# Block sums of the down-projection weights formed in HBM by accumulating DMAs, and sixteen chunk pairs as seven products in place of eight

## The reference, cut to what matters

```python
# first block, stage 0
u = causal_dwconv(h @ w_ffn_up[layer], ffn_conv_w[layer], ffn_conv_b[layer])
u_gate, u_val = jnp.split(u, 2, axis=-1)
x = x + (jax.nn.silu(u_gate) * u_val) @ w_ffn_down[layer]
# second block, stages 1 and 2
f_gate, f_up = jnp.split(h2 @ w_ffn_in[l], 2, axis=-1)
x = x + (jax.nn.silu(f_gate) * f_up) @ w_ffn_out[l]
```

## Time and profile before

| | |
|---|---|
| median of 3 runs | 1244.31 us (1244.18 to 1244.35) |
| profiled execution | 1244.18 us, its span 1242.9 us |
| PE busy | 1239.0 us (100%) |
| DVE, ACT, POOL busy | 957.8, 722.1, 422.0 us |
| DMA queue of SP | 232.67 MB, 53.4% of the 16 engines' time |
| granted TensorE clock | 1.0 throughout |

### The profile page before, as it was taken

The page is one execution under the profiler, slowest core; times in us unless marked ns, Lnnn a source line. Parts: engine busy times, 40 slices in busy tenths (PEclk is TensorE's granted clock), DMA queues, the critical chain, the costliest instruction groups (busy, mean ns, idle before and its releaser), DMA issues.

```text
span 1242.9 us, 17085 instructions
## 1 busy us (share of the span) xinstructions
PE 1239.0 (100%) x6634; PEld 1061.2 (85%) x6634; DVE 957.8 (77%) x1377; ACT 722.1 (58%) x1023; POOL 422.0 (34%) x338
## 2 busy tenths in 40 slices
PE   9999999999999999999999999999999999999999
PEld 8988788888888889888888888888988888888887
DVE  6875667677887478986878888986898597888895
ACT  7755545376765365577836555546457674655552
POOL 0010012039892069377420112008746750012100
PEclk9999999999999999999999999999999999999999
DMA  9753334555555448644554554465855454555442
GB/s 360 274 195 136 136 119 169 173 199 187 197 179 201 170 170 267 214 155 176 175 210 175 183 190 162 176 220 185 289 180 193 154 174 165 203 183 190 162 166 114
DMA packets 39008, 233.75 MB, mean 188 GB/s; under 512 B 4752, under 2 KB 5392, under 8 KB 13072
## 3 DMA queue, kind: packets, MB, share of 16 engines
q1 hardware_dynamic: 38928, 232.67, 53.4%
HBM read 225.31 MB, written 1.05 MB: 182 GB/s over the span
## 4 chain that ended last, share of the span: by engine, by line
PE 100%; DVE 0%; issue 0%; POOL 0%; POOLq 0%
PE ps L657 19%; PE ps L564 18%; PE ps L566 18%; PE ps L565 18%; PE ps L662 10%; PE ps L569 6%; PE ps L583 2%; PE ps L625 1%; PE ps L624 1%; PE ps L623 1%; PE ps L725 1%; PE ps L1209 1%; PE ps L700 0%; PE ps L893 0%; PE ps L810 0%; PE ps L811 0%
## 5 line engine op out<-in xcount | busy, mean ns | idle before, releaser
L1299 ACT ACTIVATE whi<-raw 128x2048 fp32r<-128x2048 f32 (+1 forms) x212 | 400.2, 1891 | 115.0 <-PE ps L566 101.5
L2052 DVE TENSOR_TENSOR wlo<-raw,whi 128x2048 fp32r<-128x2048 f32 x168 | 388.0, 2315 | 90.0 <-ACT whi L1299 89.3
L1885 POOL TENSOR_TENSOR wlo<-raw,whi 128x512 fp32r<-128x512 f32 x176 | 229.1, 1337 | 88.6 <-ACT whi L1299 85.6
L657 PE MATMUL ps<-hh,whi 128*128 128x512 f32 x1056 | 255.8, 391 | 0.0
L657 PEld LDWEIGHTS ps<-hh,whi 128*128 128x128 f32 x1056 | 193.0, 188 | 36.5
L564 PE MATMUL ps<-whi,hh 128*128 128x512 f32 (+1 forms) x504 | 201.3, 399 | 0.0
L566 PE MATMUL ps<-whi,hh 128*128 128x512 f32 (+1 forms) x504 | 195.5, 388 | 0.0
L565 PE MATMUL ps<-wlo,hh 128*128 128x512 f32 (+1 forms) x504 | 195.1, 387 | 0.0
L1857 POOL TENSOR_TENSOR st<-st,sm 128x1 f32<-128x1 f32 (+2 forms) x28 | 45.2, 1614 | 391.5 <-DVE st L2106 228.0
L662 PEld LDWEIGHTS ps<-hh,wlo 128*128 128x128 f32 x1056 | 137.8, 191 | 6.7
L662 PE MATMUL ps<-hh,wlo 128*128 128x256 f32 x1056 | 139.8, 282 | 0.0
(11 more groups left out here) (348 smaller groups left out, 2061.6 us busy)
## 6 DMA issues: line engine op xcount, KB each, us to landing
raw<-in_w SPq DMA_DIRECT2D x202, 1024.0 KB, 4.9
raw<-in_w SPq DMA_DIRECT2D x12, 256.0 KB, 6.7
gain<-in_bias SPq DMA_DIRECT2D x12, 256.0 KB, 5.0
kst<-kh SPq DMA_DIRECT2D x16, 128.0 KB, 2.8
qst<-qh SPq DMA_DIRECT2D x16, 128.0 KB, 2.3
raw<-in_w SPq DMA_DIRECT2D x2, 560.0 KB, 10.8
x<-in_x SPq DMA_DIRECT2D x4, 256.0 KB, 5.7
gain<-in_rows SPq DMA_DIRECT2D x2, 512.0 KB, 5.6
```

Of the source, the lines that this page charges most:

```text
L657: pe.op.matmul(o[:, :], wh[:, k, c], t.hh[:, k, :, :], start=k == 0, stop=False, skip_group_check=True)
L1299: act.op.activation(t.whi[i % NHI][:, c], t.raw[i % NRAW][:, c], ACT.Copy).then_inc(*at("act_hi", ("hi", i)))
L1885: pool.op.tensor_tensor(t.wlo[i % NRAW][:, half(k)], t.raw[i % NRAW][:, half(k)], t.whi[i % NHI][:, half(k)].bitcast(F32), ALU.subtract).t ...
L2052: dve.op.tensor_tensor(t.wlo[i % NRAW][:, c], t.raw[i % NRAW][:, c], t.whi[i % NHI][:, c].bitcast(F32), ALU.subtract).then_inc(*at("dve_lo ...
```

## The change

Sixteen pairs are made as seven products in place of eight: four in stage 0, five in stage 1, seven in stage 2. No weight sum is made by DVE. SP copies three of the four weight blocks of each pair from HBM to a tensor `sums` in HBM (two DMAs of 512 KB for a pair), and POOL issues accumulating DMAs of 256 KB that add blocks within HBM (four for a pair, in three steps with waits between them). They come in two batches: nine pairs (stages 0 and 1) with their copies ahead of the loads of chunks 16 to 24, and seven pairs (stage 2) with theirs ahead of the loads of the seven chunks from `pa0_0` on. The sum chunk of a pair is then loaded like any other, 1 MB, and of the pair's own chunk only three of four blocks are loaded, 0.75 MB. In stage 0 DVE makes the sums of `g` (`block_sums`) and their lower part, as POOL splits weights there.

```diff
+    def down(unit, name, layer):
+        n = int(unit[2])
...
+            plan.append((name, layer, cols((512, 512), (0, 512)) if c in SEVEN[n] else cols((0, 1024)), 2 * c, 2))
+            if c in SEVEN[n]:
+                plan.append((None, n, range(1024), 2 * c, 2))
...
-SEVEN = (1, 3, 5, 7)
+SEVEN = ((2, 3, 4, 6), (1, 2, 3, 4, 5), (1, 2, 3, 4, 5, 6, 7))
+BY_DVE = ((), (), ())
...
+FORMED = [i for i in sorted(SUMS) if PLAN[i][3] // 2 not in BY_DVE[PLAN[i][1]]]
+BATCH = [[i for i in FORMED if (PLAN[i][1] == 2) == late] for late in (False, True)]
+COPIES = {a + n: i for a, batch in zip((16, UNITS["pa0_0"][0]), BATCH) for n, i in enumerate(batch)}
...  sp_program
-        load(f"d_raw{i % NRAW}", t.raw[i % NRAW][:, 0:width(i)], src, ("raw", i))
+        c = slice(512 if i + 1 in FORMED else 0, width(i))
+        load(f"d_raw{i % NRAW}", t.raw[i % NRAW][:, c], src[:, c], ("raw", i))
+
+    def load_sums(i):
+        sp.wait_ge(*on("used", i - NRAW))
+        sp.wait_ge(*on("sums formed", int(i in BATCH[1])))
+        load(f"d_raw{i % NRAW}", t.raw[i % NRAW][:, :], d["sums"][FORMED.index(i)], ("raw", i))
+
+    def blocks_copied(i):
+        src = d["in_w"][OFFS[i - 1]:OFFS[i]].rearrange("(p n) -> p n", p=128)
+        for h in range(2):
+            load("d_copied", d["sums"][FORMED.index(i)][:, 1024 * h:1024 * h + 1024], src[:, 512 + 512 * h:1536 + 512 * h],
+                 *([("blocks copied", int(i in BATCH[1]))] * (h and i in (BATCH[0][-1], BATCH[1][-1]))))
...
-        if i not in SUMS:
+        if i in COPIES:
+            blocks_copied(COPIES[i])
+        if i in FORMED:
+            load_sums(i)
+        elif i not in SUMS:
             load_raw(i)
...  act_program, stage 0
+            if f % 2 and (f - 3) // 2 in SEVEN[n]:
+                sums_upper((f - 3) // 2)
...  pool_program
+    def added(sem, dst, src, *names):
+        pool.op.dma_start(dst, src, accum_op=ALU.add).then_inc(*at(sem, *names, by=16))
+
+    def first_sums(late):
+        pool.wait_ge(*on("blocks copied", late))
+        for i in BATCH[late]:
+            s = d["sums"][FORMED.index(i)]
+            first = d["in_w"][OFFS[i - 1]:OFFS[i]].rearrange("(p n) -> p n", p=128)[:, 0:512]
+            for j in range(2):
+                added("d_one", s[:, half(j)], first, *([("first sums", late)] * (j and i == BATCH[late][-1])))
+
+    def later_sums(late):
+        pool.wait_ge(*on("first sums", late))
+        for i in BATCH[late]:
+            s = d["sums"][FORMED.index(i)]
+            added("d_two", s[:, half(2)], s[:, half(0)], *([("second sums", late)] * (i == BATCH[late][-1])))
+        pool.wait_ge(*on("second sums", late))
+        for i in BATCH[late]:
+            s = d["sums"][FORMED.index(i)]
+            added("d_three", s[:, half(3)], s[:, half(2)], *([("sums formed", late)] * (i == BATCH[late][-1])))
...  behind the rope of kr, before the retention statistics
+    first_sums(0)
...  behind the retention statistics, before the powers of norm n1
+    later_sums(0)
...  behind the powers of the norm before stage 1, and around its g_sums
+        if l == 0:
+            first_sums(1)
+        for c in SEVEN[l + 1]:
             g_sums(l + 1, c)
+        if l == 0:
+            later_sums(1)
...  dve_program
-            if i + 1 in SUMS:
+            if i + 1 in SUMS and i + 1 not in FORMED:
                 weight_sums(i)
...
+            if n == 0 and f % 2 and (f - 3) // 2 in SEVEN[n]:
+                block_sums((f - 3) // 2)
+            if n == 0 and f % 2 == 0 and (f - 4) // 2 in SEVEN[n]:
+                c = (f - 4) // 2
+                lower([("g sums", n, c)], t.gsl[SEVEN[n].index(c)][:, :, :], t.gs[:, :, :],
+                      t.gsh[SEVEN[n].index(c)][:, :, :], ("g sums hi", n, c), "dve_small")
...
-            if n and c == SEVEN[-1]:
+            if c == SEVEN[n][-1]:
                 splits(i + 1 + AHEAD)
                 sevens_added(n)
...
+    sums = nc.dram_tensor("sums", (len(FORMED), 128, CW), _mybir.dt.float32, kind="Internal").ap()
```

More of the change, by code:

```diff
@@ L38, in wide @@
             plan.append((name, layer, cs, k, per))
+    def down(unit, name, layer):
+        n = int(unit[2])
+        units[unit] = []
+        for c in range(NFT // 2):
+            units[unit].append(len(plan))
+            plan.append((name, layer, cols((512, 512), (0, 512)) if c in SEVEN[n] else cols((0, 1024)), 2 * c, 2))
+            if c in SEVEN[n]:
+                plan.append((None, n, range(1024), 2 * c, 2))
     def in1(unit, a, n):
@@ L78, in chunk_plan @@
             wide(f"up{l + 1}_{f}", "w_ffn_in_2", l, cols((128 * f, 128), (FF + 128 * f, 128)), 8, 8)
[L79 to L84, removed]
+        down(f"dn{l + 1}", "w_ffn_out_2", l)
     return plan, units
-SEVEN = (1, 3, 5, 7)
+SEVEN = ((2, 3, 4, 6), (1, 2, 3, 4, 5), (1, 2, 3, 4, 5, 6, 7))
+BY_DVE = ((), (), ())
 GATES = (4, 5, 0, 1, 2, 3)
@@ L385, in place @@
     t.gs = at("gs", p + 82, [128, 4, 128])
-    t.gsh, t.gsl = ([at(f"{w}{c}", p + o + (4, 8, 40, 30)[c], [128, 4, 128], R32) for c in range(len(SEVEN))]
+    t.gsh, t.gsl = ([at(f"{w}{c}", p + o + (4, 8, 40, 34, 30, 0, 21)[c], [128, 4, 128], R32) for c in range(7)]
                     for w, o in (("gsh", 44), ("gsl", 46)))
@@ L1085, in seven @@
         def seven(c):
-            i, pair, edge = chunks[c], SEVEN.index(c), (SEVEN[0], SEVEN[-1])
+            i, pair, edge = chunks[c], SEVEN[n].index(c), (SEVEN[n][0], SEVEN[n][-1])
             pe.wait_ge(*on("lo", i))
@@ L1620, in silu, with sums_upper @@
                 *at("act_small", ("fs", n, f)))
+        def sums_upper(c):
+            upper(("g sums hi", n, c), t.gsh[SEVEN[n].index(c)][:, :, :], t.gs[:, :, :], ("g sums", n, c, "whole"))
         def out(f):
@@ L1628, in out @@
                 silu(f, "scaled")
-                if f % 2 == 0 and f // 2 - 2 in SEVEN:
-                    c = f // 2 - 2
-                    upper(("g sums hi", n, c), t.gsh[SEVEN.index(c)][:, :, :], t.gs[:, :, :], ("g sums", n, c, "whole"))
+                if f % 2 == 0 and f // 2 - 2 in SEVEN[n]:
+                    sums_upper(f // 2 - 2)
                 return
@@ L2581, in gated, with block_sums, less @@
                 *at("dve_out", ("fg", n, f)))
+        def block_sums(c):
+            k0, k1 = (t.fg[(2 * c + k) % 4] for k in range(2))
+            a11, a21, a12, a22 = k0[:, 0:128], k0[:, 128:256], k1[:, 0:128], k1[:, 128:256]
+            s3, s5, s6, s7 = (t.gs[:, j, :] for j in range(4))
+            def less(dst, a, b, names=()):
+                dve.op.tensor_tensor(dst, a, b, ALU.subtract).then_inc(*at("dve_small", *names))
+            await_own("dve_out")
+            less(s5, a21, a22)
+            less(s7, a11, a21)
+            await_own()
+            less(s6, a11, s5)
+            await_own()
+            less(s3, a12, s6, [("g sums", n, c, "whole")])
         def up_out(f):
@@ L2998 @@
     out = nc.dram_tensor("out_0", (S, D), _mybir.dt.float32, kind="ExternalOutput").ap()
-    program(nc, {**d, "out": out})
+    sums = nc.dram_tensor("sums", (len(FORMED), 128, CW), _mybir.dt.float32, kind="Internal").ap()
+    program(nc, {**d, "out": out, "sums": sums})
     r = _run(nc, [arrays], core_ids=[0])
```

24 lines of the change are left out of this document (11 added, 13 removed).

## The result

The changed kernel takes 1254.05 us (median of 5 runs, 1252.26 to 1254.59) beside 1244.18 (5 runs, 1243.77 to 1244.35) of the kernel before: ratio 1.0077, 95% interval 1.0065 to 1.0088. It is slower by 9.9 us, where 1239.5 was forecast, and lies outside the range. The profiled execution, the fastest of the five, took 1252.26 us with a span of 1250.9, 8.0 more than before.

What follows compares the result with a forecast made beforehand. PE, busy 1239.0 of 1242.9 us, bounds the kernel. 1242.9 - 5.44 (fewer matmuls) + 0.3 (loading) + 0.3 (stage 0 sums) = 1238.1 us span; with 1.3 around it and 0.1 for the median 1239.5, range 1238.3 to 1249.

Steps and rivals of the forecast that it cites:

- Stage 0's sums of `g` on DVE: Units 7 to 12 of stage 0: DVE at 22.4 of 22.5 us, falls back a little; 0 to 1 us, taken 0.3.
- The cushion: Stage 0: DVE's falling back is caught by four pairs of PSUM banks and the three chunks weights are ahead.
- Each pair of seven products: Down stages: 21 matmuls instead of 24 a pair, 24 fewer in all at 0.227 us, 5.44 us gained.
- The weight sums taken from DVE: 21 us less of DVE, worth nothing by itself; makes pairs in a row possible; counted 0.
- Issues on POOL: Accumulating DMAs cost POOL 0.33 to 2.68 us each to issue, taken 1; loss 0, barely at the high end.
- The copies: In SP's queue ahead of loads: 2.5 to 4.9 us for a MB, taken 3.3; loss 0.
- Rivals 1 to 3: Copies near 4.9 us a MB (chance 0.25); copies over 5.2 (0.13); accumulating DMAs hold queue or POOL longer (0.08).
- c: Time to copy a MB within HBM: 2.5 to 4.9 us, taken 3.3.
- late batch: At ACT's split of chunk 105: loss 6c - 25.9 us, nothing up to c = 4.3, 3.5 at 4.9.
- early batch: Chunk 24 is there at 84.5 + 9c us; costs nothing until c = 4.85, 0.4 us at 4.9.
- rival 1: Gain mostly given back to copies, c near 4.9: 1243.4 us; 1240.6 to 1244.6 for c 4.5 to 5.1; chance 0.25.
- More loading in the down stages: A pair loads 1.75 chunks in 4.76 us; only stage 2 can lose, 0 to 1.5 us, taken 0.3.

Runs made afterwards that it cites:

- the kernel with the moved adds and pair 1 by DVE: Kernel with stage 0 plain, late batch's second and third adds issued in layer 1, pair 1 of stages 1 and 2 summed by DVE: 1247.34 us.
- the kernel with stage 0 plain: Changed kernel without pairs of seven products in stage 0, stages 1 and 2 keeping their five and seven: 1243.06 us, ratio 0.9991 to before.
- the one in which POOL writes zeros: Changed kernel, POOL writing zeros in place of its weight splits of stage 0, all sixteen pairs kept: 1240.49 us, ratio 0.9969 to before.
- stage 2 alone: Kernel before with only stage 2 changed, to seven pairs with sums formed by DMAs: 1243.17 us, ratio 0.9992 to before.

## Why the prediction was wrong

**The step that failed** is "Stage 0's sums of `g` on DVE", taken as 0.3 us with an upper end of 1. It put a pair at 4 x 0.4 + 0.7 us, from POOL's 0.58 us. That row is of POOL where it does nothing else; no row of before shows a DVE operation of this shape beside POOL's splits. They meet in exactly this stage: POOL was busy for 20.40 of 22.50 us. Measured is 4.7 + 0.7 us for a pair, so two pairs in four units bring DVE to 28.5 of 22.5. The trace of before had the warning, in another operation with two SBUF inputs: in stage 0 DVE's `fg` product of 128x256, which takes 0.42 us in stage 1 (694.53 us), lasted three times as long beside POOL's splits, though not each time.
```profile
302.11 5.24 POOL L1885 TENSOR_TENSOR wlo<-raw,whi 128x512 fp32r<-128x512 f32 x4
304.88 1.31 DVE L2580 TENSOR_TENSOR fg<-fu,fs 128x256 f32<-128x256 f32 x1
```
None of the three rivals had stage 0 in it, so no chance was left for this loss, although the step itself came to 22.4 of 22.5 us. Without POOL's splits beside it the changed kernel is faster than before by 3.7 us, where 4.7 were forecast; stage 0 then brings its 2.7 us in full.

**The cushion was misread.** The step let the banks and the chunks ahead catch what DVE is late. But ACT stands directly behind DVE's wide operation in each unit, and the sums were put ahead of that: moving them alone brought 5.5 us.

**No term for the clock.** Two waits of over 3 us each cost 1.7 us more at 1.2 GHz. Not every wait does so: the one of 2.27 us in the same trace, and that of 3.51 us in the kernel with the moved adds and pair 1 by DVE, were followed by the full clock.

**Steps that held.** Each pair of seven products brings 0.67 to 0.68 us where nothing waits. The weight sums taken from DVE bring nothing by themselves, and pairs in a row need them gone. Issues on POOL were taken at 1 us, with 0 in all; they took 0.82 to 0.85, and PE waits for none of them in the changed kernel. They do cost about 2.2 us when put elsewhere. The copies were taken at 3.3 us for a MB; measured are 3.0 between the first chunks and 3.4 over the nine (they land 5.9 us apart), and no wait of PE follows, as forecast: ACT's split of chunk 105, at 641.30 us, starts on PE and not on a landing. An estimate from the 207 to 214 GB/s of the Trainium skill's "DMA: Bandwidth & Descriptors" (section "Latency and other measured facts") was 4.9 us; this trace does not agree, but the page's copies were of 16 KiB a partition with rows at least 512 KiB apart, and these are of 4 KB, 8 KB apart. Twice the copies in the same place come to 4.2 each, which leaves it open what a queue of nothing but copies does. Rivals 1 to 3 did not happen.

**Two slips in the sums**, without effect on the outcome. At c = 5.1 the formulas give 6 x 5.1 - 25.9 = 4.7 us for the late batch and 84.5 + 9 x 5.1 - 128.2 = 2.2 for the early one, so rival 1 ends at 1246.4 and not at 1244.6. And the sum without its two losses is 1238.9, not 1238.4.

**A size that was off.** "More loading in the down stages" was put at 0.3 us and bounded by 1.5. In the profiled execution of the changed kernel `dn1` and `dn2` fall short of their matmuls by 0.2 us together. With the same stages 1 and 2 they fall short by 0.5 and 1.0 in the kernel with stage 0 plain and by 0.8 and 0.5 in the one in which POOL writes zeros: near the upper end. 0.7 us of it is there with stage 2 alone. Why it varies so between executions wasn't followed.

Left open: the sums of `g` of stage 0 on an engine other than DVE, or POOL's splits held back while they run, wasn't tried.

## What to carry to other kernels

Price an operation from a row of the same engine, with the same number of SBUF inputs and the same neighbour at work; here the row of an idle stretch (0.29 us) was a quarter of the price (1.16). Where no row has the same shape, look for any operation of that kind in the same stage, and compare it with itself in a stage where the neighbour rests. An engine's share says nothing where two engines meet: add a stage's small operations with the length of the neighbour's, put them behind whatever another engine is waiting for, and spread them so that the units between can make them up. And where consecutive gains load one queue, the last one of a run may bring nothing: try the run with one fewer, or with a gap.

## What the runs showed of the hardware

A 128x128 subtraction on DVE, with both inputs in SBUF, takes 0.29 us with POOL idle and 0.71 to 1.38 (mean 1.16) beside POOL's splits, where it lasts about as long as they do. The `fg` product goes from 0.42 to 0.77 us on average. Where DVE's split of 128x2048 started first, POOL's `glo` took 2.30 us instead of 0.74. Beside a POOL instruction that only writes, that DVE split takes its usual 2.29 us. One DVE product of 128x256 took 7.57 us instead of 0.42 beside POOL's DMA issues and splits. A DMA issued by POOL costs it 0.82 to 0.85 us. Copies in HBM ahead of loads in one queue take 3.0 to 3.4 us for a MB when one stands before each load, and 4.2 when two do (with 2.5 us for the load).
